# Key pages of a paged decode attention requested by SyncE, between its weights and values, instead of by GpSimd

## The reference

```
xn = rms_norm(x, g_mix)
q, k, v, f_logit, xl, gl = split(xn @ w_in)          # 8 heads of 128, 8 recurrent blocks of 128
past_k = cache_k[page_table]                          # per sequence 16 pages x 128 rows x (8 x 128)
past_v = cache_v[page_table]
s = q.k / sqrt(128) + (Fq - Fk)                       # F: running sum of log-forget values
att = softmax(s) @ v
lru = gelu(gl) * rg_lru(causal_conv(xl))
x = x + concat(rms_norm(att), rms_norm(lru)) @ w_out
x = x + square(relu(rms_norm(x) @ w_up)) @ w_down
```

## Time and profile before

| | |
|---|---|
| median of 3 runs | 2656.99 us |
| lowest, highest | 2656.24, 2664.38 us |
| profiled execution, span | 2659.0 us |
| TensorE busy with matmuls | 2540.2 us, 96% |
| VectorE, ScalarE, GpSimd busy | 1194.3, 691.8, 287.8 us |
| steps 0 to 7 of the loop | about 158 to 854 us |
| read from HBM | 338.49 MB |

### The profile page before, as it was taken

How to read it: one execution, slowest core, us unless ns; L and a number is a source line. 1 busy time by engine, 2 the same in 40 slices (tenths; PEclk the granted TensorE clock), 3 DMA queues, 4 the chain that set the end, 5 groups by cost and what they waited for, 6 DMA issues and landing times.

```text
span 2659.0 us, 51148 instructions
## 1 busy us (share of the span) xinstructions
PE 2540.2 (96%) x20297; PEld 2494.4 (94%) x20297; DVE 1194.3 (45%) x1358; ACT 691.8 (26%) x797; POOL 287.8 (11%) x249
## 2 busy tenths in 40 slices
PE   6997999999988979999999999999999999999997
PEld 5997899899888879999999999999999999999997
DVE  5356797779777442253333323333233333332332
ACT  5222323332332232232122122121121221221233
POOL 0033243234323001100000000000000000000011
PEclk9998999999999689999999999999999999999998
DMA  6365786678666343333332232322332323223322
GB/s 203 96 192 184 237 272 227 225 247 271 228 217 214 111 131 85 89 81 94 94 95 95 81 93 95 87 87 95 95 94 88 86 95 95 81 93 95 95 80 80
DMA packets 388832, 352.30 MB, mean 132 GB/s; under 512 B 13635, under 2 KB 337636, under 8 KB 387476
## 3 DMA queue, kind: packets, MB, share of 16 engines
q1 hardware_dynamic: 361716, 279.65, 34.6%
q0 software_dynamic: 18608, 67.64, 7.5%
q10 hardware_dynamic: 8448, 4.20, 0.5%
HBM read 338.49 MB, written 12.94 MB: 132 GB/s over the span
## 4 chain that ended last, share of the span: by engine, by line
PE 65%; DMA 1%; DVE 1%; issue 0%; ACT 0%; DVEq 0%; SPq 0%; ACTq 0%; POOL 0%; PEldq 0%; POOLq 0%
PE PS L1326 41%; PE PS L1330 21%; PE PS L1449 1%; DMA VR<-in_cache_v 1%; PE PS L1365 1%; DMA RAW<-in_w_out 0%; PE PS L1673 0%; PE PS L1599 0%; PE PS L1469 0%; DVE KR L919 0%; DVEq L893 0%; PE PS L1470 0%; PE PS L1458 0%; DVE WL L882 0%; PE PS L1480 0%
## 5 line engine op out<-in xcount | busy, mean ns | idle before, releaser
L1326 PE MATMUL PS<-XH,WH 128*128 128x260 f32 x3872 | 822.4, 294 | 15.8 <-DVE WL L882 6.0
L1330 PE MATMUL PS<-XH,WL 128*128 128x260 f32 x3872 | 820.1, 294 | 0.0
L1326 PE MATMUL PS<-XL,WH 128*128 128x260 f32 x3872 | 788.2, 286 | 0.0
L1326 PEld LDWEIGHTS PS<-XH,WH 128*128 128x128 f32 x3872 | 604.8, 192 | 18.4 <-DVE WL L882 7.9
L1330 PEld LDWEIGHTS PS<-XH,WL 128*128 128x128 f32 x3872 | 606.2, 192 | 0.0
L1326 PEld LDWEIGHTS PS<-XL,WH 128*128 128x128 f32 x3872 | 604.6, 191 | 0.0
L882 DVE TENSOR_TENSOR WL<-RAW,WH 128x2048 fp32r<-128x2048 f32 x185 | 428.8, 2318 | 259.3 <-ACT WH L549 259.1
L549 ACT ACTIVATE WH<-RAW 128x2048 fp32r<-128x2048 f32 x185 | 354.2, 1915 | 604.1 <-PE PS L1330 600.3
L1326 PE MATMUL PS<-HH,WH 128*128 128x260 f32 x2048 | 413.6, 283 | 0.0
L1330 PE MATMUL PS<-HH,WL 128*128 128x260 f32 x2048 | 412.9, 283 | 0.0
L1326 PE MATMUL PS<-HL,WH 128*128 128x260 f32 x2048 | 412.4, 283 | 0.0
(11 more groups left out here) (261 smaller groups left out, 1280.7 us busy)
## 6 DMA issues: line engine op xcount, KB each, us to landing
KR<-in_cache_k POOLq DMA_DIRECT2D x128, 512.0 KB, 5.4
VR<-in_cache_v SPq DMA_DIRECT2D x256, 256.0 KB, 3.8
RAW<-in_w_up SPq DMA_DIRECT2D x128, 512.0 KB, 4.8
RAW<-in_w_down SPq DMA_DIRECT2D x128, 512.0 KB, 4.3
RAW<-in_w_in SPq DMA_DIRECT2D x82, 512.0 KB, 5.1
RAW<-in_w_out SPq DMA_DIRECT2D x32, 512.0 KB, 5.0
xT_spill<-A SPq DMA_DIRECT2D x1, 4160.0 KB, 13.4
XT<-in_x_prompt SPq DMA_DIRECT2D x4, 1024.0 KB, 7.5
```

The source lines that it names most:

```text
L1326: mm(dsts[c], wh(k), x[:, k, c * HT:(c + 1) * HT], start=first and n == 0 and x is xh, stop=False)
L1330: ins = mm(dsts[c], wl(k), xh[:, k, c * HT:(c + 1) * HT], start=False, stop=last and n == len(kts) - 1)
```

## The change

Key pages are asked for by SyncE. The first four pages stand ahead of step 0. In quarters 1 to 3 of a step the load of page b = 4q + part stands after the half weight unit (if there is one in this part) and ahead of the value halves of the same part. Pages 0 to 3 of the next sequence stand at the end of the step. Each waits for the same count of `k_scored` as before, now on SyncE. GpSimd is left with its products and the maximum, and its loop runs over all 8 steps without peeled ones.

```diff
@@ SyncE
+            def load_keys(i, b, first=False):
+
+                g = page(i, b)
+                if not first or b >= NKS:
+                    sp.wait_ge(k_scored, NPG * i + b - NKS + 1)
+                sp.dma_start(KR[:, b % NKS, :], k_pages[one(g), :, :].rearrange("a p f -> p (a f)")).then_inc(k_full[b % NKS], 16)
+
             def step(i, head, prev, nxt, first_v=False):
...
                             if part % 2 == 0:
                                 load_part(slot, src, part // 2)
+                        if head and q:
+                            load_keys(i, K_Q * q + part, not prev)
                         if prev:
                             b = K_Q * q + part
                             value_half(i - 1, b, 1, first_v)
...
+                if head and nxt:
+                    for b in range(NKS):
+                        load_keys(i + 1, b)
...
+            for b in range(NKS):
+                load_keys(0, b, True)
             step(0, True, False, True)
@@ GpSimd
-            def load_keys(i, b):
...
-            def step(i, first, last):
+            def step(i):
 
                 for m in range(NPG // 2):
-                    def loads():
-                        for b in (2 * m + 2, 2 * m + 3):
-                            if last and b >= NPG:
-                                continue
-                            if not first or b >= NKS:
-                                pool.wait_ge(k_scored, NPG * i + b - NKS + 1)
-                            load_keys(i, b)
-                    loads()
                     if m == 0:
                         pool.wait_ge(qb_ready, i + 1)
...
-            load_keys(0, 0)
-            load_keys(0, 1)
-            step(0, True, False)
-            with pool.Fori(1, NB - 1) as i:
-                step(i, False, False)
-            step(NB - 1, False, True)
+            with pool.Fori(0, NB) as i:
+                step(i)
```

More of the change, by code:

```diff
@@ L480, in _ @@
                                     bass.IndirectOffsetOnAxis(ap=IDX[:, 0:1], axis=0)).then_inc(gather_in, 16)
-            def load_keys(i, b):
-                g = pool.value_load(PGT[0:1, one(i * NPG + b)], min_val=0, max_val=cache_k.shape[1] - 1)
-                pool.dma_start(KR[:, b % NKS, :], k_pages[one(g), :, :].rearrange("a p f -> p (a f)")).then_inc(k_full[b % NKS], 16)
-            def step(i, first, last):
+            def step(i):
                 for m in range(NPG // 2):
-                    def loads():
-                        for b in (2 * m + 2, 2 * m + 3):
-                            if last and b >= NPG:
-                                continue
-                            if not first or b >= NKS:
-                                pool.wait_ge(k_scored, NPG * i + b - NKS + 1)
-                            load_keys(i, b)
-                    loads()
                     if m == 0:
@@ L509, in _ @@
             pool.wait_ge(state_ready, 2)
-            pool.wait_ge(pgt_in, 16)
-            load_keys(0, 0)
-            load_keys(0, 1)
-            step(0, True, False)
-            with pool.Fori(1, NB - 1) as i:
-                step(i, False, False)
-            step(NB - 1, False, True)
+            with pool.Fori(0, NB) as i:
+                step(i)
             def accumulate(n):
```

## The result

The changed kernel takes 2725.85 us in the median of 4 runs (2723.17 to 2728.78), the kernel before 2660.68 in 4 runs. The ratio is 1.025, with a 95% interval of 1.023 to 1.027: 2.5% slower. The forecast was 2712 us, with a range of 2681 to 2739.

A forecast was written before the change was run, and what follows sets the result against it. TensorE (busy 96%) bounds the kernel, with VectorE's chain pacing the ends of steps. Steps 2 to 7 +54.0, step 1 +5.3, step 0 -4: +55 us, 2659.0 to 2714 profiled, median 2712 us; range 2681 to 2739.

The forecast's parts named there:

- The wait on SyncE: Start of quarter 1: SyncE stops at key page 4 until page 0 is summed, with value page 4 queued behind.
- TensorE's stop, 5.7 us: Quarter 1, steps 2 to 7: TensorE waits 5.7 us a step for late value page 4 (4.4 to 9.2).
- the lock: Rival: early product 3 stretches VectorE's multiply of page 0 by 2.2 us, delaying SyncE and TensorE; 2727 to 2739, chance 0.18.
- the main case: TensorE's stop for value page 4 plus a low-clock window behind it: 2695 to 2725 us, chance 0.55.
- The clock, 3.3 us: Behind the stop for value page 4, TensorE loses 3.3 us a step to a window of lower granted clock.
- TensorE's wait for the exponential stays at 4.3: End of steps 2 to 7: VectorE's chain moves by TensorE's full 9.0 us, so the 4.3 us wait absorbs nothing.
- VectorE's three holds: VectorE delayed by older value page 14 (5.2 us late), row maxima awaiting scores, and third unit's low part awaiting its high part.
- Step 1, +5.3: Step 1: a stop of 2.0 us for value page 4 plus 3.3 us for the clock.
- Step 0, -4: Step 0, bound by VectorE: earlier GpSimd products save 4 us, the middle of 0 to 8.
- The faster one: Rival: SyncE's waits are hidden and VectorE's 27.3 us wait for products comes off: 2630 us, chance 0.07.
- The one without the clock: Rival: quarter 1 stop is real but TensorE keeps its clock, or page 4 lands fastest: 2681 to 2689, chance 0.15.
- the rule that the issuer decides only the sequencer's time: All issuers' DMAs end on the same 16 DMA engines; by this alone the change would be worth nothing.

The follow-up runs named there:

- the first experiment: Kernel before, key loads still on GpSimd, plus one SyncE wait in quarter 1 ahead of the value halves until page 0 is scored: 2708.1 us, ratio 1.018.
- the second: Changed kernel with only key page 4's load moved behind the two value halves of its part: 2668.1 us, ratio to before 1.002.
- the kernel with both moves: Changed kernel with page 4's key load behind its part's values and keys 0 to 3 asked for in quarter 0, behind the values: 2645.7 us, ratio 0.995.
- products tied: Kernel before, with GpSimd's product of page 2m+1 held until VectorE has made its product of page 2m: 2680.1 us, ratio 1.008.

## Why the prediction was right, and where its terms were off

The sign, the mechanism and the range held; the median was 14 us over the forecast, half a percent.

**The wait on SyncE** was right in every link, and the first experiment shows it alone, the second shows its absence. The release, an assumed 0.2 us, was 0.17 in step 5 (page 0 summed at 644.61, key page 4 asked for at 644.78).

**TensorE's stop, 5.7 us**, was mis-sized. It is 7.2 to 8.3 us in five steps and 3.56 in step 6, 41.8 in all where six times 5.7 are 34.2. The price of the request and landing was near (644.6 to 649.35 is 4.7 us, forecast 5.1); what was off is the time of page 0, 2.4 us behind TensorE's need where the forecast had 0.6. The forecast had the lock as another case, with chance 0.18 and 2.2 us a step. It came, with a whole 2.1 us, in five of the six steps, but not with the late products of pages 13 and 15 that this rival also counted (VectorE's wait for products is 24.4 us, less than before). The outcome, 2726, lies just above the main case (2695 to 2725) and just under this rival's (2727 to 2739).

**The clock, 3.3 us**, was right in size. TensorE's busy time rose from 511.7 to 530.6 over steps 2 to 7, 3.2 a step. The granted clock alone would say more: (1 - 0.88) x 103.6 less (1 - 0.96) x 89.3 is 8.9 us for step 5, of which the work shows 4.4. Part of the low window lies over TensorE's standing and costs nothing: at the start of step 5 TensorE stands from 614.7 to 620.1, and the granted clock is 0.50, the lower level of 1.2 GHz, from 616.9 on. The window, for the earlier trace rows, and the first 8.5 us behind the stop for value page 4:

```profile
616.90:627.10 10.20, 7.00 (x32) 7.03 (x33) 3.35 (x12) 7.63 (x11) 0.39 (x1) 0.50 0.46 126
649.48:658.00 8.52, 8.52 (x35) 8.16 (x36) 7.03 (x8) 0.00 (x0) 2.37 (x1) 0.51 0.89 279
```

The second of these windows has no counterpart in the kernel before; it is the one that the prediction asked for.

**That TensorE's wait for the exponential stays at 4.3** was wrong. It rose from 25.4 to 33.4 over the six steps, +8.0. Two things act here. It also rose to 33.2 with the added wait alone, where the maximum stayed at 6.5 to 6.9 us: there VectorE's chain is held longer than TensorE. And the maximum over partitions rose by 1.9, which the prediction put at nothing ("starts when VectorE is ready, as before"): it starts so, but takes longer beside the key pages. With this alone, the key of page 4 behind its values, the wait is 32.9. So either makes nearly the whole rise, and both together make no more; how they share it is not shown. Moving keys 0 to 3, which shortens the stops too, takes the wait to 24.7.

By the clock of TensorE the six steps then add up: 41.8 + 8.0 + 18.9 = 68.7 against 67.8 measured and 54.0 forecast. Of the 11 us by which the whole missed (55 forecast, 66.0 between the spans), the stops made +7.6, the waits for the exponential +8.0, the clock -0.9, step 1 -3.4 and step 0 +0.9; these come to 12.2, 1 us more than there is.

**The end of the step and VectorE's three holds.** All three are there. The older value page is late by 4.50 where 5.2 was forecast, the row maxima wait 4.17 for the scores, and the low part of the third unit 2.55 for its high part, where it was 0.70; the last two rows:

```profile
661.46 0.62 DVE L1128 TENSOR_REDUCE NM<-PS 128x1 f32<-128x128 f32 x2 [4.17 <-PE PS L1467]
...
684.19 2.29 DVE L878 TENSOR_TENSOR WL<-RAW,WH 128x2048 fp32r<-128x2048 f32 x1 [2.55 <-ACT WH L545]
```

**Step 1, +5.3**, was +1.9: a stop of 3.51 and no more low clock than before (0.94 and 0.93), and 2.0 us of it came off the wait for the exponential (4.36 for 6.36). **Step 0, -4**, was -3.1: the maximum there took 10.1 instead of 6.5, so that the products' gain was about 6.7 us, within the bounds of 0 to 8, if nothing else moved in step 0, and half of it was given back.

**The rivals.** The faster one fell with its condition: value page 4 landed some 7 us after TensorE wanted it (649.35 against 642.2). The one without the clock fell with TensorE's busy time. Of the rule that the issuer decides only the sequencer's time (the Trainium skill, DMA: Bandwidth & Descriptors, section Issuing engines are not separate DMA queues) the kernel with both moves shows the range: same queues for the same bytes, 80 us apart by the place of five loads in SyncE's order.

## What to carry to other kernels

Before moving a DMA to another engine's queue, write down the semaphore it waits for and what stands behind it there; a wait that was harmless on a queue with nothing urgent behind it is charged to everything urgent behind it on the new one. If the move is wanted for other reasons, put the request behind the issues whose slots come free first, one by one and not as a rule for all, since the reverse order can starve the moved loads. And when a stall is triggered by a step of another engine, look for what stretches that step: here two collisions of 2.1 us each made a stop of 4 us into one of 8.

## What the runs showed of the hardware

- VectorE's wait for the maximum over partitions on GpSimd took 6.4 to 7.05 us at the ends of steps 1 to 7 where no key pages had just been asked for, and 8.3 to 8.8 us at the ends of steps 1 to 6 of the changed kernel, where four of 512 KB had (7.7 to 9.7 in the two other kernels that ask for them there). Moving the loads brought it back. The trace records only a piece of 0.39 us of it, the same in all kernels; the rest shows as VectorE's wait. The table in the Trainium skill, SBUF — State Buffer, section Who interferes with whom, gives DMAs ports of their own, apart from all engines; by that alone the maximum would not have felt the loads. The measurement differs, and which part of the operation feels them stays open.
- Four small VectorE operations with three SBUF operands take 1.13, 3.25 or 5.37 us beside no, one or two products of GpSimd of 2.4 us. The delay comes in steps of 2.1 us, one for each product. Where the products began just as the additions ended, they were stretched instead, 5.84 us for two where 4.84 is usual.
- Key pages issued by SyncE landed in 4.5 us in the median and value pages in 3.4, where in the kernel before, with keys on GpSimd, it was 5.4 and 3.8: the loads landed sooner and the kernel was slower. That the issuer makes this is not shown, since with keys still on GpSimd the keys also landed in 4.8 us (wait alone) and 4.6 (products tied). What did change with the issuer is the queue that the page lists: software_dynamic carried 67.64 MB before and 0.52 MB after, hardware_dynamic q1 279.65 and 346.77 MB.
